# Statistics of every second tile of the last LayerNorm on ScalarE

## The chip, the cores and the metric

The kernel runs on one core of a Trainium2 chip. A time is the device time of one execution in microseconds; lower is better. It was taken in three runs, and one further execution was profiled.

## What is computed

One step of a streaming encoder layer for 1024 prompt tokens and 128 sample tokens with 1024 features: an input projection, three branches (a gated linear recurrence, stick-breaking attention, an mLSTM), their merging, a LayerNorm, a mixture of 32 experts of which each token takes four, and a second LayerNorm. The change concerns the second LayerNorm alone. In the reference it is the last line of the layer:

```
def _layer_norm(x, g, b):
    xf = x.astype(F32)
    mu = jnp.mean(xf, axis=-1, keepdims=True)
    var = jnp.mean(jnp.square(xf - mu), axis=-1, keepdims=True)
    return ((xf - mu) * lax.rsqrt(var + LN_EPS) * g.astype(F32) + b.astype(F32)).astype(x.dtype)
...
    x = _layer_norm(DN_ALPHA * x + f + ple, ln2_g, ln2_b)
```

All of it is computed in float32.

## The kernel before

The program is a row of stages. The last one, `stage_experts`, gathers the rows of each block of expert slots, multiplies them with that expert's two weights on TensorE, and adds the results with an indirect DMA to `residual_scratch` in DRAM, which then holds the sum `DN_ALPHA * x + f + ple`. When the last such DMA has landed, the class `LastNorm` works on the sum: 1152 tokens as NT = 9 tiles of 128 tokens (partitions) by 1024 features. Its tile `res` is the old place of the expert weights and of `xT` in on-chip memory, so the profile calls it `xT_then_expert_w`; the rows of gain and shift vectors (`norm`) stand in the first half of `expert_w`.

There is no planner. Each engine has its own instruction list, written out in program order, and semaphores tie the lists together:

- SyncE (`sync`) issues the nine loads of `res` one after the other, and then, for each tile, waits for `y_ready` and issues the store of that tile.
- VectorE (`vector`) makes, for each tile i, the statistics in `moments`: two `bn_stats` over 512 features each (L3788), one `bn_aggr` that gives mean and variance (L3791), then, once ScalarE has put the standard deviation in the variance's place, its reciprocal (L3793) and the shift -mean/std (L3796, a `scalar_tensor_tensor` of 128x1). After the moments of tile i it multiplies tile i-1 by the gain (L3807). So the statistics of a tile stand ahead of the gain of the tile before it.
- ScalarE (`scalar`) loads the table for the square root once and then makes, for each tile, the root of variance plus epsilon (L3824) and normalizes the tile in place (L3826: scale 1/std, bias -mean/std).
- GpSimd (`gpsimd`) adds the shift vector to each tile (L3815), after which the tile may be stored.

The tile `y` (`expert_y`) holds an expert block's results until they are added to DRAM. It is not used any more when `LastNorm` starts.

Of the kernel before, what the change touches and what calls it, by code (L numbers as in the profile page):

```python
# [29 lines left out]
ALU = mybir.AluOpType  # L30
ACT = mybir.ActivationFunctionType
AX_X = mybir.AxisListType.X

P = 128
D = 1024
# [5 lines left out]
NT = T // P  # L41
# [39 lines left out]
@contextmanager  # L81
def stage_semaphores(nc):

    owned = []

    def sem(name):
        owned.append(nc.alloc_semaphore(name))
        return owned[-1]

    yield sem  # L90
    nc.clear_and_free_semaphores(owned)
    nc.all_engine_barrier()
# [6 lines left out]
class WeightStream:  # L99
# [5 lines left out]
    def __init__(self, nc, ctx, g):  # L105
        self.nc = nc
        self.source = g.w_in[0].rearrange("(k p) n -> p k n", p=P)
        raw = ctx.enter_context(nc.sbuf_tensor("w_stream", [P, self.RAW * 512], F32, side="right"))
        hi = ctx.enter_context(nc.sbuf_tensor("w_stream_high", [P, self.WR * 512], F32R, side="right"))
        lo = ctx.enter_context(nc.sbuf_tensor("w_stream_low", [P, self.WR * 512], F32R, side="right"))  # L110
        self.raw, self.hi, self.lo = (t[:].rearrange("p (s n) -> p s n", n=512) for t in (raw, hi, lo))
        self.a_raw, self.a_hi, self.a_lo = (t[:, 0:3 * DT * P].rearrange("p (s k c) -> p s k c", s=3, k=DT)
                                            for t in (raw, hi, lo))
        sem = ctx.enter_context(stage_semaphores(nc))
        self.a_in = [sem(f"a_w_in{i}") for i in range(3)]
        self.a_high = sem("a_w_high")
        self.a_split = sem("a_w_split")
        self.a_done = sem("a_proj_done")
        self.v_in = [sem(f"v_w_in{i}") for i in range(self.RAW)]
        self.v_high = sem("v_w_high")  # L120
        self.v_split = sem("v_w_split")
        self.v_free = sem("v_w_free")
        self.m_prod = sem("m_prod")
        self.b_prod = sem("b_prod")
# [3145 lines left out]
def stage_experts(nc, g):  # L3270
# [20 lines left out]
    with ExitStack() as ctx:  # L3291
        sem = ctx.enter_context(stage_semaphores(nc))
        def sb(name, shape, dt=F32):
            return ctx.enter_context(nc.sbuf_tensor(name, shape, dt))
# [3 lines left out]
        w2 = sb("expert_w2", [P, FT, D])  # L3298
# [18 lines left out]
        y = sb("expert_y", [P, 2, D])  # L3317
# [28 lines left out]
        y_left = sem("e_y_left")  # L3346
        y_low = sem("e_y_low")
        waits_passed = sem("e_waits_passed")
        last_norm = LastNorm(nc, ctx, sem, g, w2[:, 0:2, :])
        block = ctx.enter_context(nc.Block())  # L3350

        def full_turns(eng):
# [390 lines left out]
class LastNorm:  # L3743


    def __init__(self, nc, ctx, sem, g, norm):
        def sb(name, shape):
            return ctx.enter_context(nc.sbuf_tensor(name, shape, F32))

        self.nc, self.g, self.norm = nc, g, norm  # L3750
        self.res = g.rows[:].rearrange("p (i d) -> p i d", i=NT)
        self.stats = sb("ln2_stats", [P, NT, 2, 6])
        self.mv = sb("ln2_mean_var", [P, NT, 2])
        self.shift = sb("ln2_shift", [P, NT, 1])
        self.root = sb("root_of_eps", [P, 1])
        self.norm_in = sem("k_norm_in")
        self.res_in = [sem(f"k_res_in{i}") for i in range(NT)]
        self.all_out = sem("k_all_out")
        self.stat_ready = sem("k_stat_ready")
        self.var_ready = sem("k_var_ready")  # L3760
        self.std_ready = sem("k_std_ready")
        self.rstd_ready = sem("k_rstd_ready")
        self.shift_ready = sem("k_shift_ready")
        self.hat_ready = sem("k_hat_ready")
        self.scaled = sem("k_scaled")
        self.y_ready = sem("k_y_ready")
        self.y_out = sem("k_y_out")
# [15 lines left out]

    def moments(self, dve, i):
        nc, mv = self.nc, self.mv
        dve.wait_ge(self.res_in[i], 16)
        for half in range(2):
            nc.vector.bn_stats(self.stats[:, i, half, :], self.res[:, i, half * 512:(half + 1) * 512]  # L3788
                               ).then_inc(self.stat_ready, 1)
        dve.wait_ge(self.stat_ready, 2 * i + 2)  # L3790
        nc.vector.bn_aggr(mv[:, i, :], self.stats[:, i].rearrange("p a b -> p (a b)")).then_inc(self.var_ready, 1)  # L3791
        dve.wait_ge(self.std_ready, i + 1)
        nc.vector.reciprocal(mv[:, i, 1:2], mv[:, i, 1:2]).then_inc(self.rstd_ready, 1)  # L3793

        dve.wait_ge(self.rstd_ready, i + 1)
        nc.vector.scalar_tensor_tensor(out=self.shift[:, i, :], in0=mv[:, i, 0:1], scalar=-1.0, in1=mv[:, i, 1:2],  # L3796
                                       op0=ALU.mult, op1=ALU.mult).then_inc(self.shift_ready, 1)

    def vector(self, dve):
        for i in range(NT + 1):  # L3800
            if i < NT:
                self.moments(dve, i)
            if i == 1:
                dve.wait_ge(self.norm_in, 32)
            if i:
                dve.wait_ge(self.hat_ready, i)
                self.nc.vector.tensor_tensor(self.res[:, i - 1, :], self.res[:, i - 1, :], self.norm[:, 0, :],  # L3807
                                             ALU.mult).then_inc(self.scaled, 1)
# [9 lines left out]
    def scalar(self, act):  # L3818
        nc, mv = self.nc, self.mv

        nc.scalar.activation(self.root[:], self.g.eps[:], ACT.Sqrt)
        for i in range(NT):
            act.wait_ge(self.var_ready, i + 1)
            nc.scalar.activation(mv[:, i, 1:2], mv[:, i, 1:2], ACT.Sqrt, bias=self.g.eps[:]).then_inc(self.std_ready, 1)  # L3824
            act.wait_ge(self.shift_ready, i + 1)
            nc.scalar.activation(self.res[:, i, :], self.res[:, i, :], ACT.Identity, bias=self.shift[:, i, :],  # L3826
                                 scale=mv[:, i, 1:2]).then_inc(self.hat_ready, 1)


def build_program(nc, i, o):  # L3830
# [20 lines left out]
    with ExitStack() as ctx:  # L3851
# [12 lines left out]
        with ExitStack() as trunk:  # L3864
# [14 lines left out]
            with ExitStack() as early:  # L3879
# [43 lines left out]
                with ExitStack() as pieces:  # L3923
# [6 lines left out]
                    stage_out(nc, g, xT, xT, out_early, route)  # L3930
                stage_route(nc, g, xT, route)
        stage_experts(nc, g)


# [20 lines left out]
```

## Time and profile before

| | us |
|---|---|
| three runs: median (lowest to highest) | 2656.44 (2656.16 to 2660.66) |
| profiled execution: its time | 2657.0 |
| profiled execution: span of its instructions | 2655.3 |
| start of the first load of `LastNorm`, from the span's start | 2607.39 |
| start of the first and end of the last GpSimd add | 2616.24, 2647.09 |

All times in the profile count from the span's start. An engine is busy while it executes an instruction; a wait inside an instruction counts as busy too. In the lists in order of time a row has start, duration, engine, line, operation, output and inputs, and in square brackets the time for which the engine was idle before it and what ended that. Starts and durations there are rounded to 0.01 us.

### The profile page before, as it was taken

The numbers are of one execution on the slowest core, as the hardware profiler recorded it, in microseconds if no ns is written. First come the engines' busy times: TensorE is split into PE (matmuls) and PEld (weight loads), VectorE is DVE, ScalarE is ACT, GpSimd is POOL, SyncE is SP. The second block draws the span as 40 slices with busy tenths as digits, with TensorE's granted clock in tenths as the row PEclk, the third lists the DMA queues.
The fourth block names the chain that finished last, engine by engine and source line by source line (L and its number), as shares of the span: only waits on it lengthen the run. The fifth ranks groups of instructions, "written<-read, shape, count | busy, mean of one in ns | idle before, by whom it ended". The sixth has DMA issues, their size and how long they took to land. (4 is left out here: it accounts for less than half of the span.)

```text
span 2655.3 us, 40268 instructions
## 1 busy us (share of the span) xinstructions
PE 2459.5 (93%) x14944; PEld 2220.1 (84%) x14944; DVE 1595.9 (60%) x2515; ACT 1313.5 (49%) x2098; POOL 671.3 (25%) x496
## 2 busy tenths in 40 slices
PE   7999999998878899999999989799999999999991
PEld 6988797896657899999988667688898999999991
DVE  3665331217658554444535476578788788877775
ACT  4566330115435544334322222467777677777662
POOL 1000100004302011010113214244444444544433
PEclk8999999999999899999999999899999999999995
DMA  8321233203387565565544322788998898988864
GB/s 249 90 67 43 80 100 104 83 20 127 110 292 180 127 163 134 131 163 141 136 123 148 124 77 75 242 280 276 288 289 280 275 280 283 292 259 282 275 195 170
DMA packets 389291, 468.10 MB, mean 176 GB/s; under 512 B 17326, under 2 KB 312458, under 8 KB 389167
## 3 DMA queue, kind: packets, MB, share of 16 engines
q1 hardware_dynamic: 367069, 395.82, 47.7%
q0 software_dynamic: 17760, 60.34, 9.0%
q10 hardware_dynamic: 4338, 10.23, 1.0%
q8 instruction: 85, 1.39, 0.2%
q14 instruction: 39, 0.32, 0.0%
HBM read 397.63 MB, written 68.71 MB: 176 GB/s over the span
## 5 line engine op out<-in xcount | busy, mean ns | idle before, releaser
L3523 PE MATMUL banks<-slot_rowsT,expert_w_high 128*128 128x288 f32 (+2 forms) x2048 | 561.4, 356 | 5.4 <-DVE expert_w_low L3661 4.7
L3526 PE MATMUL banks<-slot_rowsT,expert_w_low 128*128 128x144 f32 (+2 forms) x2048 | 494.0, 241 | 0.0
L3526 PEld LDWEIGHTS banks<-slot_rowsT,expert_w_low 128*128 128x128 f32 x2048 | 399.9, 195 | 1.4
L3523 PEld LDWEIGHTS banks<-slot_rowsT,expert_w_high 128*128 128x128 f32 x2048 | 394.2, 192 | 7.5 <-DVE expert_w_low L3661 5.0
L3577 ACT CAST expert_w_high<-xT_then_expert_w 128x2048 fp32r<-128x2048 f32 x127 | 235.6, 1903 | 2.9 <-DMA xT_then_expert_w<-in_exp_w 2.9
L3661 DVE TENSOR_TENSOR expert_w_low<-xT_then_expert_w,expert_w_high 128x2048 fp32r<-128x2048 f32 x95 | 214.5, 2285 | 17.0 <-ACT expert_w_high L3577 17.0
L3444 POOL TENSOR_TENSOR expert_w_low<-xT_then_expert_w,expert_w_high 128x2048 fp32r<-128x2048 f32 x32 | 146.6, 4582 | 207.5 <-ACT expert_w_high L3577 207.5
L2246 PE MATMUL banks<-xT_chunk_high,w_gates_high 128*128 128x384 f32 x576 | 193.7, 336 | 4.5 <-DVE xT_chunk_low L2318 4.5
L2247 PE MATMUL banks<-xT_chunk_low,w_gates_high 128*128 128x384 f32 x576 | 193.5, 336 | 0.0
L2248 PE MATMUL banks<-xT_chunk_high,w_gates_low 128*128 128x384 f32 x576 | 193.4, 336 | 0.0
L3702 DVE TENSOR_TENSOR expert_w_low<-expert_w,expert_w_high 128x1024 fp32r<-128x1024 f32 x128 | 159.2, 1243 | 51.7 <-ACT expert_w_high L3605 51.7
L2366 POOL TENSOR_TENSOR xT_then_expert_w<-xT_then_expert_w,gate_sigmoid 128x384 f32<-128x384 f32 x48 | 56.5, 1176 | 488.4 <-DVE gate_sigmoid L2357 488.4
L3594 ACT ACTIVATE low_part_and_bias<-banks,expert_b 128x192 f32<-128x192 f32 x256 | 93.8, 418 | 108.0 <-PE banks L3526 107.7
L2283 ACT CAST w_gates_high<-w_gates 128x1024 fp32r<-128x1024 f32 x72 | 75.7, 1052 | 130.9 <-PE banks L2258 130.0
L3469 POOL DMA_INDIRECT residual_scratch<-expert_y,slot_rows_out x64 | 123.2, 1924 | 49.0 <-POOL slot_rows_out L3437 28.2
L3605 ACT CAST expert_w_high<-expert_w 128x1024 fp32r<-128x1024 f32 x128 | 132.2, 1033 | 1.0 <-DMA expert_w<-in_exp_w 1.0
L2258 PE MATMUL banks<-yT_chunk_high,w_proj_low 128*128 128x384 f32 x384 | 128.3, 334 | 0.0
L2256 PE MATMUL banks<-yT_chunk_high,w_proj_high 128*128 128x384 f32 x384 | 128.3, 334 | 0.0
L2257 PE MATMUL banks<-yT_chunk_low,w_proj_high 128*128 128x384 f32 x384 | 128.3, 334 | 0.0
L2333 DVE TENSOR_TENSOR w_gates_low<-w_gates,w_gates_high 128x1024 fp32r<-128x1024 f32 x72 | 109.2, 1516 | 31.4 <-ACT w_gates_high L2283 31.2
L3688 DVE TENSOR_TENSOR gate_and_up<-banks,low_part_and_bias 128x384 f32<-128x384 f32 x128 | 71.0, 555 | 93.9 <-ACT low_part_and_bias L3594 93.3
L2357 DVE TENSOR_TENSOR gate_sigmoid<-gate_sigmoid,banks 128x384 f32<-128x384 f32 x48 | 26.6, 554 | 160.8 <-PE banks L2258 160.8
(552 smaller groups left out, 6184.0 us busy)
## 6 DMA issues: line engine op xcount, KB each, us to landing
xT_then_expert_w<-in_exp_w SPq DMA_DIRECT2D x126, 1024.0 KB, 7.8
expert_w<-in_exp_w SPq DMA_DIRECT2D x32, 2048.0 KB, 9.4
w_gates<-in_w_in SPq DMA_DIRECT2D x72, 512.0 KB, 4.4
cached_k<-in_cache_sb_k SPq DMA_DIRECT2D x16, 1024.0 KB, 10.1
cached_v<-in_cache_sb_v SPq DMA_DIRECT2D x16, 1024.0 KB, 10.2
w_stream<-in_w_in SPq DMA_DIRECT2D x48, 256.0 KB, 4.2
w_proj<-in_w_pa SPq DMA_DIRECT2D x24, 512.0 KB, 5.1
w_stream<-in_w_in SPq DMA_DIRECT2D x16, 512.0 KB, 5.4
```

The source lines that it names most:

```text
L2246: nc.tensor.matmul(gate, hi, x_hi[:, k, :], start=(k == 0), stop=False)
L2247: nc.tensor.matmul(gate, hi, x_lo[:, k, :], start=False, stop=False)
L2248: last = nc.tensor.matmul(gate, lo, x_hi[:, k, :], start=False, stop=(k == DT - 1))
L2256: nc.tensor.matmul(proj, hi, y_hi[:, first + k, :], start=(k == 0), stop=False)
L2257: nc.tensor.matmul(proj, hi, y_lo[:, first + k, :], start=False, stop=False)
L3444: pool.tensor_tensor(w1_chunk(w1_lo, FT - 1), w1_chunk(w1, FT - 1), w1_chunk(w1_hi, FT - 1).bitcast(F32), ALU.subtract).then_inc(w1_last_s ...
L3523: nc.tensor.matmul(out[:, 0:2 * SLOTS].rearrange("p (a s) -> p a s", a=2)[:, :, 0:width], hi, xgT[:, par, k, :, 0:width], start=(place == ...
L3526: last = nc.tensor.matmul(out[:, 0:width], lo, xgT[:, par, k, 0, 0:width], start=False, stop=(place == DT - 1), skip_group_check=True)
L3577: nc.scalar.copy(w1_chunk(w1_hi, f), w1_chunk(w1, f)).then_inc(w1_high, 1)
L3605: nc.scalar.copy(w2_hi[:, f, :], w2[:, f, :]).then_inc(w2_high, 1)
L3661: nc.vector.tensor_tensor(w1_chunk(w1_lo, f), w1_chunk(w1, f), w1_chunk(w1_hi, f).bitcast(F32), ALU.subtract).then_inc(w1_split, 1)
L3702: nc.vector.tensor_tensor(w2_lo[:, f, :], w2[:, f, :], w2_hi[:, f, :].bitcast(F32), ALU.subtract).then_inc(w2_split, 1)
```

## The change

For odd tiles (1, 3, 5, 7) the statistics move from VectorE to ScalarE. ScalarE reads the tile with an identity activation that also sums along the features, turns the sum into -mean with a 128x1 copy, and reads the tile again with a square activation whose bias is -mean and which also sums; the root of the odd tile then takes this sum with scale 1/1024. The passes' elementwise output goes to `y[:, 0, :]` and is not read. Since an odd tile's mean has its sign turned, its shift is taken with +1 instead of -1. Even tiles keep `bn_stats` and `bn_aggr` on VectorE.

The order on both engines changes too. On VectorE `moments` is split: `factors(i)` (reciprocal and shift) comes first, then the statistics of tile i+1 (only if that is even), and then the gain of tile i-1. On ScalarE the two passes of tile i+1 stand between the root of an even tile i and its normalizing.

```diff
-        last_norm = LastNorm(nc, ctx, sem, g, w2[:, 0:2, :])
+        last_norm = LastNorm(nc, ctx, sem, g, w2[:, 0:2, :], y[:, 0, :])
...
+        self.sums = sb("ln2_sums", [P, NT, 2])
+        self.pass_out = pass_out
...
     def moments(self, dve, i):
         nc, mv = self.nc, self.mv
-        dve.wait_ge(self.res_in[i], 16)
-        for half in range(2):
-            nc.vector.bn_stats(...)
-        dve.wait_ge(self.stat_ready, 2 * i + 2)
-        nc.vector.bn_aggr(mv[:, i, :], ...).then_inc(self.var_ready, 1)
+        if i % 2 == 0:
+            dve.wait_ge(self.res_in[i], 16)
+            for half in range(2):
+                nc.vector.bn_stats(...)
+            dve.wait_ge(self.stat_ready, i + 2)
+            nc.vector.bn_aggr(mv[:, i, :], ...).then_inc(self.var_ready, 1)
+
+    def factors(self, dve, i):
+        nc, mv = self.nc, self.mv
         dve.wait_ge(self.std_ready, i + 1)
         nc.vector.reciprocal(mv[:, i, 1:2], mv[:, i, 1:2]).then_inc(self.rstd_ready, 1)
         dve.wait_ge(self.rstd_ready, i + 1)
-        nc.vector.scalar_tensor_tensor(out=self.shift[:, i, :], in0=mv[:, i, 0:1], scalar=-1.0, ...)
+        nc.vector.scalar_tensor_tensor(out=self.shift[:, i, :], in0=mv[:, i, 0:1], scalar=1.0 if i % 2 else -1.0, ...)
 
     def vector(self, dve):
+        self.moments(dve, 0)
         for i in range(NT + 1):
             if i < NT:
-                self.moments(dve, i)
+                self.factors(dve, i)
+            if i + 1 < NT:
+                self.moments(dve, i + 1)
             if i == 1:
                 dve.wait_ge(self.norm_in, 32)
             if i:
                 dve.wait_ge(self.hat_ready, i)
...
         nc.scalar.activation(self.root[:], self.g.eps[:], ACT.Sqrt)
+        def sums(i):
+            act.wait_ge(self.res_in[i], 16)
+            nc.scalar.activation(self.pass_out, self.res[:, i, :], ACT.Identity, accum_out=self.sums[:, i, 0:1]
+                                 ).then_inc(self.sum_ready, 1)
+            act.wait_ge(self.sum_ready, i)
+            nc.scalar.activation(mv[:, i, 0:1], self.sums[:, i, 0:1], ACT.Copy, scale=-1.0 / D
+                                 ).then_inc(self.mean_ready, 1)
+            act.wait_ge(self.mean_ready, i // 2 + 1)
+            nc.scalar.activation(self.pass_out, self.res[:, i, :], ACT.Square, bias=mv[:, i, 0:1],
+                                 accum_out=self.sums[:, i, 1:2]).then_inc(self.sum_ready, 1)
         for i in range(NT):
-            act.wait_ge(self.var_ready, i + 1)
-            nc.scalar.activation(mv[:, i, 1:2], mv[:, i, 1:2], ACT.Sqrt, bias=self.g.eps[:]).then_inc(self.std_ready, 1)
+            if i % 2 == 0:
+                act.wait_ge(self.var_ready, i // 2 + 1)
+                nc.scalar.activation(mv[:, i, 1:2], mv[:, i, 1:2], ACT.Sqrt, bias=self.g.eps[:]
+                                     ).then_inc(self.std_ready, 1)
+                if i + 1 < NT:
+                    sums(i + 1)
+            else:
+                act.wait_ge(self.sum_ready, i + 1)
+                nc.scalar.activation(mv[:, i, 1:2], self.sums[:, i, 1:2], ACT.Sqrt, bias=self.g.eps[:], scale=1.0 / D
+                                     ).then_inc(self.std_ready, 1)
             act.wait_ge(self.shift_ready, i + 1)
             nc.scalar.activation(self.res[:, i, :], self.res[:, i, :], ACT.Identity, bias=self.shift[:, i, :],
                                  scale=mv[:, i, 1:2]).then_inc(self.hat_ready, 1)
```

## Rows read from the trace of the kernel before

**Rows 1.** The page, busy time, share of the span and instructions of each engine

```profile
PE 2459.5 (93%) x14944; PEld 2220.1 (84%) x14944; DVE 1595.9 (60%) x2515; ACT 1313.5 (49%) x2098; POOL 671.3 (25%) x496
```

**Rows 2.** Table by stretches: stretch, its length, busy us (instructions) of each engine

```profile
2607.39:2616.24 8.85, 0.00 (x0) 0.00 (x0) 4.85 (x12) 3.07 (x4) 0.00 (x1) 0.50 0.86 322
2616.24:2647.09 30.85, 0.00 (x0) 0.00 (x0) 25.25 (x43) 10.75 (x14) 21.06 (x9) 0.50 0.49 197
```

**Rows 3.** Instructions in order of time, one turn of the last norm

```profile
2619.65 1.27 DVE L3788 BATCH_NORM_STATS2 ln_stats<-xT_then_expert_w 128x6 f32<-128x512 f32 x2
2619.81 2.34 POOL L3815 TENSOR_TENSOR xT_then_expert_w<-xT_then_expert_w,expert_w 128x1024 f32<-128x1024 f32 x1 [1.23 <-DVE xT_then_expert_w L3807]
...
2621.53 0.16 DVE L3793 RECIPROCAL ln_mean_var<-ln_mean_var 128x1 f32<-128x1 f32 x1 [0.36 <-ACT ln_mean_var L3824]
2621.73 0.44 DVE L3796 SCALAR_TENSOR_TENSOR ln_shift<-ln_mean_var 128x1 f32<-128x1 f32 x1
2622.09 1.21 DVE L3807 TENSOR_TENSOR xT_then_expert_w<-xT_then_expert_w,expert_w 128x1024 f32<-128x1024 f32 x1
...
2623.23 1.27 DVE L3788 BATCH_NORM_STATS2 ln_stats<-xT_then_expert_w 128x6 f32<-128x512 f32 x2
2623.38 2.34 POOL L3815 TENSOR_TENSOR xT_then_expert_w<-xT_then_expert_w,expert_w 128x1024 f32<-128x1024 f32 x1 [1.23 <-DVE xT_then_expert_w L3807]
```

**Rows 4.** Instructions in order of time, before the first add

```profile
2612.09 0.29 ACT L3824 ACTIVATE ln_mean_var<-ln_mean_var,ln_eps 128x1 f32<-128x1 f32 x1 [11.62 <-DVE ln_mean_var L3791]
...
2612.69 1.28 DVE L3788 BATCH_NORM_STATS2 ln_stats<-xT_then_expert_w 128x6 f32<-128x512 f32 x2
...
2614.86 1.23 DVE L3807 TENSOR_TENSOR xT_then_expert_w<-xT_then_expert_w,expert_w 128x1024 f32<-128x1024 f32 x1
...
2616.24 2.34 POOL L3815 TENSOR_TENSOR xT_then_expert_w<-xT_then_expert_w,expert_w 128x1024 f32<-128x1024 f32 x1 [13.20 <-DVE xT_then_expert_w L3807]
```

**Rows 5.** Line L3796: count, ns least/median/most, first and last start

```profile
L3796 DVE SCALAR_TENSOR_TENSOR ln_shift<-ln_mean_var x9: 159/439/515, 2612.6 to 2639.6; 128x1 f32<-128x1 f32 x9
```

**Rows 6.** Instructions in order of time, the last multiply

```profile
2641.25 2.34 POOL L3815 TENSOR_TENSOR xT_then_expert_w<-xT_then_expert_w,expert_w 128x1024 f32<-128x1024 f32 x1 [1.23 <-DVE xT_then_expert_w L3807]
2641.34 3.33 DVE L3807 TENSOR_TENSOR xT_then_expert_w<-xT_then_expert_w,expert_w 128x1024 f32<-128x1024 f32 x1 [0.17 <-ACT xT_then_expert_w L3826]
```

**Rows 7.** Chain of waits in order of time: start, us on the chain, what

```profile
2622.17 1.14 DVE xT_then_expert_w L3807
2623.30 1.21 DVE ln_stats L3788 x2
...
2624.53 0.22 DVE ln_mean_var L3791
```

**Rows 8.** ScalarE by line from 2598 on: count, busy us, mean ns, idle before

```profile
L3826 ACT ACTIVATE xT_then_expert_w<-xT_then_expert_w,ln_shift,ln_mean_var 128x1024 f32<-128x1024 f32 x9 | 11.2, 1241 | 5.9 <-DVE ln_shift L3796 5.9
L3824 ACT ACTIVATE ln_mean_var<-ln_mean_var,ln_eps 128x1 f32<-128x1 f32 x9 | 2.6, 294 | 21.2 <-DVE ln_mean_var L3791 21.2
L3821 ACT ACT_TABLE_LOAD x1 | 1.3, 1283 | 0.0
L3637 ACT ACTIVATE expert_y<-banks,slot_gates 128x512 f32<-128x512 f32 x2 | 1.3, 683 | 0.0
L3821 ACT ACTIVATE root_of_eps<-ln_eps 128x1 f32<-128x1 f32 x1 | 0.2, 203 | 0.0
```

**Rows 9.** The page's costliest groups: the cast of expert weights on ScalarE

```profile
L3605 ACT CAST expert_w_high<-expert_w 128x1024 fp32r<-128x1024 f32 x128 | 132.2, 1033 | 1.0 <-DMA expert_w<-in_exp_w 1.0
```

**Rows 10.** Instructions in order of time, an earlier stage

```profile
958.20 1.01 POOL L2366 TENSOR_TENSOR xT_then_expert_w<-xT_then_expert_w,gate_sigmoid 128x384 f32<-128x384 f32 x1 [5.57 <-DVE gate_sigmoid L2357]
958.23 2.06 DVE L2333 TENSOR_TENSOR w_gates_low<-w_gates,w_gates_high 128x1024 fp32r<-128x1024 f32 x1
```

**Rows 11.** Line L2333: count, ns least/median/most, first and last start

```profile
L2333 DVE TENSOR_TENSOR w_gates_low<-w_gates,w_gates_high x72: 1212/1717/2065, 877.7 to 1365.9; 128x1024 fp32r<-128x1024 f32 x72
```

**Rows 12.** The nine loads of the last norm (L3776)

```profile
DMA to landing us min/median/max: 4.2/8.1/10.4
```

More of the change, by code:

```diff
@@ L3743, with __init__ @@
 class LastNorm:
-    def __init__(self, nc, ctx, sem, g, norm):
+    def __init__(self, nc, ctx, sem, g, norm, pass_out):
         def sb(name, shape):
@@ L3755, in __init__ @@
         self.root = sb("root_of_eps", [P, 1])
+        self.sums = sb("ln2_sums", [P, NT, 2])
+        self.pass_out = pass_out
+        self.sum_ready = sem("k_sum_ready")
+        self.mean_ready = sem("k_mean_ready")
         self.norm_in = sem("k_norm_in")
@@ L3785, in moments @@
         nc, mv = self.nc, self.mv
-        dve.wait_ge(self.res_in[i], 16)
-        for half in range(2):
-            nc.vector.bn_stats(self.stats[:, i, half, :], self.res[:, i, half * 512:(half + 1) * 512]
-                               ).then_inc(self.stat_ready, 1)
-        dve.wait_ge(self.stat_ready, 2 * i + 2)
-        nc.vector.bn_aggr(mv[:, i, :], self.stats[:, i].rearrange("p a b -> p (a b)")).then_inc(self.var_ready, 1)
+        if i % 2 == 0:
+            dve.wait_ge(self.res_in[i], 16)
+            for half in range(2):
+                nc.vector.bn_stats(self.stats[:, i, half, :], self.res[:, i, half * 512:(half + 1) * 512]
+                                   ).then_inc(self.stat_ready, 1)
+            dve.wait_ge(self.stat_ready, i + 2)
+            nc.vector.bn_aggr(mv[:, i, :], self.stats[:, i].rearrange("p a b -> p (a b)")).then_inc(self.var_ready, 1)
+    def factors(self, dve, i):
+        nc, mv = self.nc, self.mv
         dve.wait_ge(self.std_ready, i + 1)
@@ L3795, in moments @@
         dve.wait_ge(self.rstd_ready, i + 1)
-        nc.vector.scalar_tensor_tensor(out=self.shift[:, i, :], in0=mv[:, i, 0:1], scalar=-1.0, in1=mv[:, i, 1:2],
-                                       op0=ALU.mult, op1=ALU.mult).then_inc(self.shift_ready, 1)
+        nc.vector.scalar_tensor_tensor(out=self.shift[:, i, :], in0=mv[:, i, 0:1], scalar=1.0 if i % 2 else -1.0,
+                                       in1=mv[:, i, 1:2], op0=ALU.mult, op1=ALU.mult).then_inc(self.shift_ready, 1)
     def vector(self, dve):
+        self.moments(dve, 0)
         for i in range(NT + 1):
             if i < NT:
-                self.moments(dve, i)
+                self.factors(dve, i)
+            if i + 1 < NT:
+                self.moments(dve, i + 1)
             if i == 1:
```

## The prediction

> **What bounds the kernel now.** I read the page's head first, then three stretches of the end, then the chain of waits, then the end's instructions in order of time, and last single lines. The page's head is the frame and a trap: TensorE is busy for 93% of the span [rows 1], but this change lies wholly behind its last matmul. The table by stretches shows that end [rows 2]: 8.85 us from the first load's issue to GpSimd's first add, 30.85 us in which the nine adds run, and behind them the last store and the closing. No TensorE work is in either, so what is added there is added to the time one for one.
>
> In the 30.85 us VectorE is busy for 25.25 and GpSimd for 21.06 [rows 2]; VectorE looks like the bound. The instructions in order of time say otherwise. One tile's turn is 3.57 us: GpSimd's adds start at 2619.81 and 2623.38 [rows 3]. Inside it the statistics of the next tile run beside the add and are over early; VectorE's tiny `ln_shift` (L3796, 128x1) starts at 2621.73, takes 0.44 instead of 0.16, and ends at 2622.17, when the add that began at 2619.81 ends (2622.15) [rows 3]. Over all nine the median is 439 ns, the least 159 [rows 5]. The last gain multiply (L3807) shows the same at full size: it begins 0.09 after an add and takes 3.33, ending 1.08 after that add, where others take 1.21 [rows 3, 6]. `bn_stats` (1.27) and the reciprocal (0.16) keep their durations under the add (two statistics took 1.28 where none was running) [rows 3, 4]. So a VectorE instruction with two SBUF inputs stands still while GpSimd adds, and one with a single input doesn't. The turn is add 2.34, end of the shift 0.02, multiply 1.14 (from the shift's end, as the chain of waits has it), hand-over 0.08: 3.58 [rows 3, 7]. Nine adds and eight such steps of 1.24 are 31.0 against 30.85 in rows 2. The bound is add and multiply taking turns on something that both need; the statistics hide under the add.
>
> **The change part by part.** Four tiles (1, 3, 5, 7) lose two `bn_stats` and one aggregate on VectorE: 1.21 + 0.24 each in the chain [rows 7]. For tiles 3, 5 and 7 that work lay under an add, so its removal is worth nothing by itself. ScalarE gains for each a summing pass, a 128x1 copy and a squaring pass. VectorE's order changes too: before, `moments(i)` was statistics, reciprocal, shift of one tile; now the reciprocal and shift of tile i+1 stand ahead of the statistics of tile i+2. This reordering is what costs.
>
> *The filling.* The first multiply now waits for tile 1's factors, whose statistics ScalarE makes after tile 0's root at 2612.38 [rows 4]. No row has a pass with a summed output. Its bounds are the 128x1024 cast without operand pointers, 1.03 [rows 9], and the normalizing pass with two, 1.24 [rows 8], each possibly with one more 128x1 activation for the sum, 0.29 [rows 4]; I take 1.13 for the sum and 1.14 for the square, since the instructions have the cast's size and at most one pointer. The copy lies between 0.20 [rows 8] and 0.29; I take 0.25. The steps, with 0.03 at each hand-over (the shift starts 0.04 after the reciprocal's end, 2621.69 [rows 3]): sum 1.13, copy 0.28, square 1.17, tile 0's normalizing 1.14 and tile 1's root 0.19 (each started 0.1 early, as two evictions of 683 ns are busy for 1.3 together [rows 8]), reciprocal 0.19, shift 0.19, tile 2's `bn_stats` 1.21 and aggregate 0.24, multiply 1.14, hand-over 0.08. Sum 6.96; the first add stood 0.15 behind its multiply instead of 0.08 [rows 4], which is 0.07 more, and I allow 0.2 for two or three waits of ScalarE on itself, which no row has: the first add starts at about 2612.38 + 7.23 = 2619.6, where it started at 2616.24. Filling: +3.4. With passes of 1.03 and no such allowance it is +3.0, with passes of 1.24 + 0.29 it is +4.2. Tile 1's load is there by then: its `bn_stats` at 2612.69 met no wait [rows 4], so the pass at 2612.4 waits at most 0.3.
>
> *The turns.* After the multiply of tile i-1 VectorE goes straight to the reciprocal and the shift of tile i+1. An instruction without a wait starts 0.08 before the multiply's end is recorded (2623.23 against 2623.30) [rows 3]; the reciprocal takes 0.16 and the hand-over 0.03, so the shift starts 0.12 after the multiply's end, and the add 0.08 after it. The shift is 0.04 late. In the nearest case in this trace a VectorE subtraction started 0.03 after a GpSimd product (958.23 against 958.20) and took 2.06 [rows 10], where its line's least is 1212 ns [rows 11]. So the shift loses: it waits for the add's end. That hurts nobody where no statistics follow. Where i+2 is even, `bn_stats` and aggregate of tile i+2 are queued behind the blocked shift; they can run only after the add, and the next multiply, and with it the next add, is behind them. What lay under the add for nothing is now on the path at 1.21 + 0.24 = 1.45 [rows 7]. This happens for the statistics of tiles 4, 6 and 8; tile 2's is in the filling. 3 x 1.45 = +4.35. If the pairs overlap a little it is 1.40, if the multiply starts afresh 1.53: 4.2 to 4.6.
>
> The Trainium skill, "SBUF — State Buffer", section "SBUF: two separate sides", has a rule for such a meeting: whichever of GpSimd and a VectorE instruction with two SBUF inputs starts first keeps their common port for its whole length. The 2.06 agrees with it. By the rule the recorded starts alone decide, and 0.04 late gives the sum below in every turn; by the row alone no more is known than that 0.03 late was lost once.
>
> For an odd tile i+1 the loss is surer: its root comes behind the even tile's normalizing pass, which waits for that tile's shift, so its reciprocal starts some 0.4 after the multiply.
>
> *ScalarE* has room. Between an even tile's aggregate and its shift's end lie multiply 1.14, hand-over 0.08, add 2.34 and 0.02, in all 3.58; root, sum, copy and square need 2.9. A further 1.8 is free because the odd tile's shift must wait for the next add's end anyway. So 2.5 us of dearer passes in each pair would cost nothing in the turns, only in the filling.
>
> *The end.* The last multiply waits for tile 8's normalizing, which waits for a shift that no statistics precede: it starts just behind the add of tile 7 as before and stands still once [rows 6]. Store and closing are as before. The loads landed 4.2 to 10.4 after their issue, half of them within 8.1 [rows 12]. Only tile 3 is wanted sooner than before, at some 2618.5 instead of 2619.65 [rows 3]; as the fourth of nine issued one after the other from 2607.39 [rows 2] it should be there.
>
> **Sum.** +3.4 + 4.35 = +7.75, from +7.2 to +8.8. The profiled execution took 2657.0 (span 2655.3 and 1.7 around it), so 2664.75; the median of the three runs, 2656.44, lies 0.56 lower, so 2664.2.
>
> **Rivals.**
>
> *The shift slips in ahead of the add.* Then the statistics run under the add as before, and odd tiles' factors are in time as well, since ScalarE's pair of tiles takes 0.29 + 2.58 + 1.14 + 0.19 + 1.24 = 5.4 of 7.15 us. Only the filling remains: 2656.4 + 3.4 = 2659.8, which is +0.13% and so not slower by the bound that I use: 0.2%, 5.3 us, about what a measurement of this kernel can tell from no change. For it: 0.04 us is little, and it decides as soon as the shift starts no later than the add takes hold. Against it: 0.03 late was lost [rows 10].
>
> *VectorE's own time is the bound after all.* Then the three odd turns shrink until GpSimd's add limits them, from 3.57 to 2.42: 3 x 1.15 = -3.45, which the filling of +3.4 eats: 2656.4, no change. For it: VectorE's 25.25 busy of 30.85 [rows 2]. Against it: 0.28 of each shift is waiting, and the 3.33 of the last multiply. The Trainium skill's "Perfetto Trace Analysis", section "Optimizing Scalar/DVE Operations", advises moving work to ScalarE when VectorE is saturated, and warns of its shared port with GpSimd; by its first half this rival would come, by its warning mine.
>
> *The table is loaded anew for the squaring pass and again for the root.* Two loads of 1.283 [rows 8] for each odd tile: 2.57 in the filling, and 0.1 above the 2.5 free in each of three turns, so some +2.8 more: 2667.0. Against it: nine identity passes alternate with nine roots behind a single load in this stretch [rows 8]; no square is seen there. The Trainium skill's "ScalarE: Activation LUTs", section "Table sets: the hidden batching unit", says that cheap functions are in every set, which speaks against this rival.
>
> **Numbers.** The forecast 0.72, the shift in time 0.13, VectorE as bound 0.05, tables 0.07, something unseen 0.03. The forecast alone would be 2663.2 to 2665.6; with tables it reaches 2667. Leaving out the rival at 2659.8 would leave out more than 0.2, so the range is 2659.3 to 2667.3. Slower by over 0.2%: the forecast less the tenth of it that scatter may push under 5.3 us, and tables: 0.74. Within 0.2%: 0.23. Faster: 0.03, since no case reaches -5.3.
>
> **What the profile after would show.** First add near 2619.6. GpSimd's adds 3.57 and 5.0 us apart by turns, three times 5.0. Shifts of 1.7 to 2.3 us, each ending with an add. `bn_stats` of tiles 4, 6, 8 after the add and not beside it. No table load after L3821's. I am wrong if all distances are 3.57 (the shift was in time), if they are under 3.5 in odd turns (VectorE was the bound), or if ScalarE's passes exceed 1.5.

## The result and the profile after

The changed kernel is slower. Its median over 19 runs is 2661.21 us, that of the kernel before over 19 runs beside it 2656.16, which is 5.05 less. The ratio of the two kernels, formed from all these runs, is 1.0026 with a 95% interval from 1.0014 to 1.0037, which is 6.9 us, from 3.7 to 9.8. The forecast was +7.75; the range held the median and the sign was right. That the kernel is slower by over 0.2% is likely but not shown, since 1.002 lies inside the interval.

The page's head of the profiled execution:

```profile
span 2664.3 us, 40276 instructions
...
PE 2459.5 (92%) x14944; PEld 2218.4 (83%) x14944; DVE 1602.8 (60%) x2503; ACT 1323.9 (50%) x2118; POOL 668.7 (25%) x496
```

The span grew by 9.0, but not all of that is the change's. The first load of the last norm is issued at 2609.20, where it was issued at 2607.39 before, and nothing ahead of it differs in the program: in the profiled executions of this study that moment lies anywhere from 2599.32 to 2612.63. So the runs below are compared by the stretch from that issue to the end of the last full-size instruction of the norm, and by the closing behind it, both read from the trace. Before, the stretch is 39.70 [rows 2], now it is 46.86. That is +7.15 (before rounding).

The table by stretches of the changed kernel, cut as in [rows 2] at the first add:

```profile
2609.20:2621.11 11.91, 0.00 (x0) 0.00 (x0) 4.77 (x13) 6.55 (x12) 0.00 (x1) 0.50 0.92 355
2621.11:2656.06 34.95, 0.00 (x0) 0.00 (x0) 31.32 (x30) 16.53 (x28) 21.07 (x9) 0.50 0.34 134
```

The filling grew from 8.85 to 11.91 (+3.06), the stretch of the nine adds from 30.85 to 34.95 (+4.10). GpSimd's busy time is the same 21.07: its adds aren't slower, they stand further apart. VectorE's instructions in that stretch fell from 43 to 30 [rows 2], and yet it is busy for 31.32 instead of 25.25. The busy time that came is waiting, as the order in time shows, here two turns in place of the one in [rows 3]:

```profile
2628.32 1.17 DVE L3818 TENSOR_TENSOR xT_then_expert_w<-xT_then_expert_w,expert_w 128x1024 f32<-128x1024 f32 x1
...
2629.41 0.15 DVE L3801 RECIPROCAL ln_mean_var<-ln_mean_var 128x1 f32<-128x1 f32 x1
2629.57 2.34 POOL L3826 TENSOR_TENSOR xT_then_expert_w<-xT_then_expert_w,expert_w 128x1024 f32<-128x1024 f32 x1 [2.62 <-DVE xT_then_expert_w L3818]
...
2629.60 2.34 DVE L3804 SCALAR_TENSOR_TENSOR ln_shift<-ln_mean_var 128x1 f32<-128x1 f32 x1
...
2631.86 1.21 DVE L3818 TENSOR_TENSOR xT_then_expert_w<-xT_then_expert_w,expert_w 128x1024 f32<-128x1024 f32 x1
...
2633.15 2.34 POOL L3826 TENSOR_TENSOR xT_then_expert_w<-xT_then_expert_w,expert_w 128x1024 f32<-128x1024 f32 x1 [1.24 <-DVE xT_then_expert_w L3818]
2633.43 0.16 DVE L3801 RECIPROCAL ln_mean_var<-ln_mean_var 128x1 f32<-128x1 f32 x1 [0.36 <-ACT ln_mean_var L3855]
2633.63 1.88 DVE L3804 SCALAR_TENSOR_TENSOR ln_shift<-ln_mean_var 128x1 f32<-128x1 f32 x1
2635.43 1.27 DVE L3793 BATCH_NORM_STATS2 ln_stats<-xT_then_expert_w 128x6 f32<-128x512 f32 x2
...
2636.74 0.21 DVE L3796 BATCH_NORM_AGGREGATE ln_mean_var<-ln_stats 128x2 f32<-128x12 f32 x1
2636.86 1.17 DVE L3818 TENSOR_TENSOR xT_then_expert_w<-xT_then_expert_w,expert_w 128x1024 f32<-128x1024 f32 x1
...
2638.12 2.34 POOL L3826 TENSOR_TENSOR xT_then_expert_w<-xT_then_expert_w,expert_w 128x1024 f32<-128x1024 f32 x1 [2.62 <-DVE xT_then_expert_w L3818]
```

The adds that start at 2629.57, 2633.15 and 2638.12 are 3.58 and 4.97 apart. In both turns the shift (L3804) stands still until the add ends, 2.34 and 1.88 long for a 128x1 result. Behind the first the multiply follows at once. Behind the second come the statistics of an even tile, 2635.43 to 2636.95, beside nothing: the next multiply starts at 2636.86. In [rows 3] the same statistics ran beside the add. Line L3804 as a whole, to be held against [rows 5]:

```profile
L3804 DVE SCALAR_TENSOR_TENSOR ln_shift<-ln_mean_var x9: 158/1879/2339, 2614.4 to 2646.7; 128x1 f32<-128x1 f32 x9
```

The median shift went from 439 to 1879 ns, with only the three that start ahead of the first add at 0.16.

### The profile page after: what moved, and what is told of

Its sections match the earlier page's. It is cut to its first block and busy times, and to the rows that moved or that the text cites. A ratio compares the mean times of both kernels' runs of the same rounds, so it can differ in the third digit from the quotient of the medians.

```text
span 2664.3 us, 40276 instructions
## 1 busy us (share of the span) xinstructions
PE 2459.5 (92%) x14944; PEld 2218.4 (83%) x14944; DVE 1602.8 (60%) x2503; ACT 1323.9 (50%) x2118; POOL 668.7 (25%) x496
## 3 DMA queue, kind: packets, MB, share of 16 engines
q8 instruction: 85, 1.39, 0.2%
## 5 line engine op out<-in xcount | busy, mean ns | idle before, releaser
L2333 DVE TENSOR_TENSOR w_gates_low<-w_gates,w_gates_high 128x1024 fp32r<-128x1024 f32 x72 | 109.2, 1517 | 31.5 <-ACT w_gates_high L2283 31.2
## 6 DMA issues: line engine op xcount, KB each, us to landing
cached_k<-in_cache_sb_k SPq DMA_DIRECT2D x16, 1024.0 KB, 10.4
cached_v<-in_cache_sb_v SPq DMA_DIRECT2D x16, 1024.0 KB, 10.4
```

## The experiments

All numbers are of one profiled execution of each; the ratio to the kernel before is over several runs. Distances are between the starts of successive adds.

| run | first load to first add | distances between adds | stretch | closing | ratio to before (95%) |
|---|---|---|---|---|---|
| before | 8.85 | 3.57, last 3.50 | 39.70 | 8.19 | |
| the change | 11.91 | 3.51, then 4.96 and 3.57 by turns, last 3.50 | 46.86 | 8.22 | 1.0026 (1.0014 to 1.0037) |
| e1, order alone | 10.34 | 3.51, five of 4.96, 3.57, 3.50 | 48.05 | 8.19 | 1.0043 (1.0025 to 1.0062) |
| e2, offload alone | 10.59 | 3.57 to 3.58, last 3.50 | 41.47 | 8.22 | 1.0021 (1.0007 to 1.0034) |
| e3, shift with one input | 12.13 | 3.50 to 3.52, last 3.22 | 42.25 | 8.22 | 1.0012 (0.9997 to 1.0026) |
| e4, tiles 3, 5, 7 only | 8.98 | 3.57 to 3.58, last 3.50 | 39.86 | 8.22 | 0.9997 (0.9984 to 1.0011) |
| e5, gain in PSUM, before | 9.17 | 3.27, six of 3.34, 2.30 | 37.13 | 8.21 | 0.9990 (0.9978 to 1.0002) |
| e6, gain in PSUM, change | 12.08 | 2.32 and 3.67 to 3.76 by turns, last 2.32 and 2.30 | 37.19 | 8.22 | 1.0000 (0.9985 to 1.0015) |
| e7, two fused passes | no adds | | 30.29 | 4.40 | 0.9956 (0.9942 to 0.9971) |
| e8, e7 without offload | no adds | | 40.69 | 4.40 | 0.9995 (0.9981 to 1.0008) |
| e9, two adds on VectorE | 8.90 | 3.57 to 3.58 (seven adds) | 37.49 | 4.40 | 0.9979 (0.9967 to 0.9991) |

**e1: the order alone.** The two halves of the change were taken apart. Here VectorE's new order, without the sums and squares on ScalarE:

```diff
     def vector(self, dve):
+        self.moments(dve, 0)
         for i in range(NT + 1):
             if i < NT:
-                self.moments(dve, i)
+                self.factors(dve, i)
+            if i + 1 < NT:
+                self.moments(dve, i + 1)
```

> The kernel before (all statistics on VectorE, no passes on ScalarE) with only the change's order on VectorE: reciprocal and shift of tile i+1 ahead of the statistics of tile i+2. Measured by the stretch from the issue of the first load to the end of the last GpSimd add: 39.70 us before, 46.86 us with the whole change. Theory (the shift stands still under the add and the statistics are queued behind it): the statistics of tile 2 come into the filling (+1.45) and those of tiles 3 to 8 each lie between an add and the next multiply, 6 x 1.39; six distances between adds of 4.96, stretch about 49.4, some 0.35% slower than before. Rival (ScalarE's two passes are what makes the turns of 4.96): without the passes every distance stays at 3.57, stretch about 41.2.

One turn of it in order of time:

```profile
2630.18 1.17 DVE L3813 TENSOR_TENSOR xT_then_expert_w<-xT_then_expert_w,expert_w 128x1024 f32<-128x1024 f32 x1
...
2631.43 2.34 POOL L3821 TENSOR_TENSOR xT_then_expert_w<-xT_then_expert_w,expert_w 128x1024 f32<-128x1024 f32 x1 [2.62 <-DVE xT_then_expert_w L3813]
2631.46 2.33 DVE L3799 SCALAR_TENSOR_TENSOR ln_shift<-ln_mean_var 128x1 f32<-128x1 f32 x1
2633.71 1.27 DVE L3788 BATCH_NORM_STATS2 ln_stats<-xT_then_expert_w 128x6 f32<-128x512 f32 x2
...
2635.14 1.17 DVE L3813 TENSOR_TENSOR xT_then_expert_w<-xT_then_expert_w,expert_w 128x1024 f32<-128x1024 f32 x1
...
2636.40 2.34 POOL L3821 TENSOR_TENSOR xT_then_expert_w<-xT_then_expert_w,expert_w 128x1024 f32<-128x1024 f32 x1 [2.62 <-DVE xT_then_expert_w L3813]
```

The add runs from 2631.43 to 2633.77, the shift beside it stands still, and the statistics and the multiply come one after the other behind it: 4.97 to the next add. Five turns were so long and not six: the first shift behind a multiply got ahead of the first add (the reason stands below), so tile 3's statistics were still covered. The stretch is 48.05, 1.4 under the 49.4 expected for that reason, and far from the rival's 41.2. The new order makes the long turns without any sums or squares on ScalarE.

**e2: the offload alone.** The other half: passes on ScalarE as in the change, VectorE's order as before.

```diff
     def vector(self, dve):
-        self.moments(dve, 0)
         for i in range(NT + 1):
             if i < NT:
+                self.moments(dve, i)
                 self.factors(dve, i)
-            if i + 1 < NT:
-                self.moments(dve, i + 1)
```

> The change's passes on ScalarE, with VectorE's order as before: statistics, reciprocal and shift of tile i, then the gain of tile i-1. Theory (order): no distance of 4.96, all near 3.57; the filling loses tile 2's statistics, 11.9 - 1.45 = 10.5; stretch about 41.3, 1.6 above the kernel before (0.06%, not to be told by time). Rival (ScalarE's passes make the turns long): three distances of 4.96 stay, stretch about 45.4.

A turn in order of time, add, shift, add:

```profile
2617.06 2.35 POOL L3824 TENSOR_TENSOR xT_then_expert_w<-xT_then_expert_w,expert_w 128x1024 f32<-128x1024 f32 x1 [1.23 <-DVE xT_then_expert_w L3816]
...
2618.98 0.45 DVE L3804 SCALAR_TENSOR_TENSOR ln_shift<-ln_mean_var 128x1 f32<-128x1 f32 x1
...
2620.64 2.35 POOL L3824 TENSOR_TENSOR xT_then_expert_w<-xT_then_expert_w,expert_w 128x1024 f32<-128x1024 f32 x1 [1.23 <-DVE xT_then_expert_w L3816]
```

The distance is 3.58, and no turn is longer. The stretch is 41.47, 1.77 above the kernel before, nearly all of it in the filling (10.59 against 8.85). With the closing that is +1.8, 0.07%, which is the lower end of the measured interval.

**e3: the shift with one SBUF tensor.** One instruction differs from the changed kernel:

```diff
-        nc.vector.scalar_tensor_tensor(out=self.shift[:, i, :], in0=mv[:, i, 0:1], scalar=1.0 if i % 2 else -1.0,
-                                       in1=mv[:, i, 1:2], op0=ALU.mult, op1=ALU.mult)
+        nc.vector.tensor_scalar(self.shift[:, i, :], mv[:, i, 0:1], mv[:, i, 1:2], 1.0 if i % 2 else -1.0,
+                                ALU.mult, ALU.mult)
```

> The changed kernel with one instruction of each tile altered: the shift is a tensor_scalar with one SBUF tensor (the mean) and 1/std as a per-partition scalar, instead of a scalar_tensor_tensor with two. Order and passes stay. Theory (an instruction with two SBUF inputs stands still under the add, one with a single tensor doesn't): shifts take 0.2 everywhere, the statistics of tiles 4, 6 and 8 run under the add, distances 3.57; filling stays at 11.9; stretch about 42.7, 4.1 less than the change. Rival (VectorE's order costs whatever the shift does, or the per-partition scalar counts as a second input): shifts up to 2.3, distances of 4.96, stretch 46.9.

VectorE's multiply and shift by line (count, busy us, mean ns):

```profile
L3818 DVE TENSOR_TENSOR xT_then_expert_w<-xT_then_expert_w,expert_w 128x1024 f32<-128x1024 f32 x9 | 21.0, 2341 | 0.0
...
L3804 DVE TENSOR_SCALAR ln_shift<-ln_mean_var 128x1 f32<-128x1 f32 x9 | 1.9, 214 | 0.3
```

All nine shifts take 0.21, whether an add runs or not, and the waiting has moved to the multiply, which now takes 2.34 on average. The statistics of even tiles run under the add again, and the stretch fell by 4.6 to 42.25, a little more than the 4.1 expected, since the distances are 3.51 and not 3.57. What is left over the kernel before, 2.55, is the filling (+3.3) less the shorter distances (-0.7). So in the turns the order costs only because of how this one 128x1 instruction reads its operands. In the filling it costs whatever the shift does: 11.91 with the new order against 10.59 without it (e2), and 12.13 here.

The last distance, 3.22, shows the same meeting the other way round: here the last multiply starts 0.16 ahead of the add and takes 1.21, and it is the add that stands still, 3.25 instead of 2.34.

**e4: three tiles, order as before.** Tile 1 keeps its statistics on VectorE; tiles 3, 5 and 7 have theirs on ScalarE.

```diff
-        if i % 2 == 0:
+        if i not in (3, 5, 7):
             dve.wait_ge(self.res_in[i], 16)
```

(with the counts that the semaphores are waited for, and VectorE's order as in e2)

> VectorE's order as before, passes on ScalarE for tiles 3, 5 and 7 only; tile 1 keeps its statistics on VectorE. Theory (add and multiply take turns, statistics lie under the add): filling as before, 8.85, distances 3.57, stretch 39.7: taking statistics from VectorE is worth nothing. Rival (VectorE's own work is the bound): the three turns without statistics fall towards 2.42, stretch about 36.3.

39.86 against 39.70, every distance as before. Three tiles' statistics, 4.3 us of VectorE's work, were taken away for no gain. But this run alone doesn't say why. One of the three turns without statistics, in order of time:

```profile
2623.10 2.35 POOL L3824 TENSOR_TENSOR xT_then_expert_w<-xT_then_expert_w,expert_w 128x1024 f32<-128x1024 f32 x1 [1.24 <-DVE xT_then_expert_w L3816]
...
2625.11 0.16 DVE L3801 RECIPROCAL ln_mean_var<-ln_mean_var 128x1 f32<-128x1 f32 x1 [2.09 <-ACT ln_mean_var L3853]
2625.30 0.16 DVE L3804 SCALAR_TENSOR_TENSOR ln_shift<-ln_mean_var 128x1 f32<-128x1 f32 x1
```

VectorE is idle for 2.09 here because ScalarE's root of the odd tile comes late, and the shift starts only 0.15 before the add ends (0.22 in the first of the three turns). So ScalarE's passes would have held these turns near 3.57 even if nothing stood still. What settles it is the changed kernel's turn from 2629.57 to 2633.15, shown above: it has no statistics, its reciprocal waits for nothing, VectorE's own work in it is some 1.5, and it is 3.58 long all the same, since the shift stands still until the add ends. VectorE's own work is not the bound.

**e5: the gain vector in PSUM.** ScalarE copies the gain vector to a free pair of banks of PSUM, the on-chip memory beside SBUF, ahead of the norm, so that the multiply reads one tensor from SBUF and one from PSUM; the shift is that of e3; all else is the kernel before.

```diff
+        act.wait_ge(self.norm_in, 32)
+        for half in range(2):
+            nc.scalar.copy(self.g.bank[half][:], self.norm[:, 0, half * 512:(half + 1) * 512]).then_inc(self.gain_moved, 1)
...
-                self.nc.vector.tensor_tensor(self.res[:, i - 1, :], self.res[:, i - 1, :], self.norm[:, 0, :],
+                self.nc.vector.tensor_tensor(self.res[:, i - 1, :], self.res[:, i - 1, :], self.gain,
```

> The kernel before (all statistics on VectorE, its order) with the gain vector copied to PSUM by ScalarE ahead of the norm, so that the multiply has one SBUF input and one PSUM input, and the shift as in the run before with one SBUF tensor. Theory (two SBUF inputs are what excludes GpSimd's add): the multiply runs beside the add with some 1.25, a turn is VectorE's own chain, statistics 1.45, root 0.32, reciprocal 0.19, shift 0.2, multiply 1.2, together 3.35; the last multiply takes 1.25 instead of 3.33; stretch 8.9 + 8 x 3.35 + 2.34 = 38.0. Rival (any full-size VectorE instruction is held up by the add): distances stay at 3.5 and the last multiply at 3.3; stretch 39.5.

A shift and a multiply within a turn, and the end (two adds back to back, with the last multiply beside them), in order of time:

```profile
2622.71 0.21 DVE L3798 TENSOR_SCALAR ln_shift<-ln_mean_var 128x1 f32<-128x1 f32 x1
2622.84 1.21 DVE L3809 TENSOR_TENSOR xT_then_expert_w<-xT_then_expert_w,banks 128x1024 f32<-128x1024 f32 x1
...
2634.16 4.64 POOL L3817 TENSOR_TENSOR xT_then_expert_w<-xT_then_expert_w,expert_w 128x1024 f32<-128x1024 f32 x2 [1.00 <-DVE xT_then_expert_w L3809]
2634.26 1.22 DVE L3809 TENSOR_TENSOR xT_then_expert_w<-xT_then_expert_w,banks 128x1024 f32<-128x1024 f32 x1 [0.18 <-ACT xT_then_expert_w L3831]
```

The last multiply starts 0.10 after an add, as in [rows 6], and takes 1.22 instead of 3.33. The distances are 3.34, the time of the chain from statistics to multiply, all of it on VectorE but for ScalarE's root. It is the two SBUF inputs that exclude the add, not the size of the instruction.

**e6: the same two edits in the changed kernel.**

> The changed kernel with the same two edits (gain in PSUM, shift with one SBUF tensor). Theory: with add and multiply no longer excluding each other VectorE needs 4.7 for a pair of tiles and GpSimd 4.85, and ScalarE becomes the bound with 5.9 for a pair (two roots, sum, copy, square, two normalizing passes, two waits for a shift): 2.95 for a tile; stretch 11.9 + 8 x 2.95 + 2.34 = 37.8, 9 less than the change and 1.9 less than the kernel before. So the change's offload would then pay. Rival (the exclusion lies elsewhere): as with the one-input shift alone, 42.3.

Two of the pairs of adds in order of time (each row two adds back to back):

```profile
2621.59 4.67 POOL L3828 TENSOR_TENSOR xT_then_expert_w<-xT_then_expert_w,expert_w 128x1024 f32<-128x1024 f32 x2 [1.32 <-DVE xT_then_expert_w L3820]
...
2627.67 4.66 POOL L3828 TENSOR_TENSOR xT_then_expert_w<-xT_then_expert_w,expert_w 128x1024 f32<-128x1024 f32 x2 [1.41 <-DVE xT_then_expert_w L3820]
```

Two adds run back to back, then GpSimd waits 1.4 for the next pair: 6.08 from pair to pair, 3.04 for a tile, where 2.95 was expected. ScalarE alone doesn't hold a pair: it is idle for 0.68 of it, and the 6.08 are a loop of ScalarE's root, sum, copy, square, normalizing pass and root (4.2) and VectorE's reciprocal, shift and statistics behind them (1.9). The stretch is 37.19 against 37.8 expected, less because the last three adds run back to back; it is 9.7 under the change and 2.5 under the kernel before, though the ratio, 1.0000, doesn't show so small a gain. But e5 gets the same 37.1 without any offload: the shorter turns here (3.04 against 3.34) are eaten by the longer filling (12.08 against 9.17).

**e7: two fused passes, no add on GpSimd.** Since add and multiply take turns at 2.34 + 1.14, the add is cheaper on VectorE itself, and with mean and 1/std as per-partition scalars the normalizing pass goes as well.

```diff
+            nc.vector.scalar_tensor_tensor(out=self.res[:, i, :], in0=self.res[:, i, :], scalar=mv[:, i, 0:1],
+                                           in1=self.norm[:, 0, :], op0=ALU.subtract if i in self.ON_DVE else ALU.add,
+                                           op1=ALU.mult).then_inc(self.scaled, 1)
...
+            nc.vector.scalar_tensor_tensor(out=self.res[:, i, :], in0=self.res[:, i, :], scalar=mv[:, i, 1:2],
+                                           in1=self.norm[:, 1, :], op0=ALU.mult, op1=ALU.add).then_inc(self.y_ready, 1)
```

> A version that removes GpSimd's add: VectorE makes two scalar_tensor_tensor passes for each tile, (x - mean) * gain and then (that * 1/std) + shift vector; ScalarE makes no normalizing pass but sums and squares of all tiles except 0 and 4, whose statistics VectorE makes; GpSimd does nothing in the norm. Same outputs. Theory: nothing contends with VectorE, whose work is 9 x (1.14 + 0.17 + 1.14) + 2 x 1.45 = 25; ScalarE 7 x 3.0 = 21 is beside it but sets when a tile may start; from the issue of the first load to the last VectorE pass about 28.5, against 39.7 before and 46.9 with the change; 0.4% faster than before. Rival (a pass with a per-partition scalar and two inputs is dearer than the multiply, up to twice): stretch 39 or more.

The two passes by line:

```profile
L3819 DVE SCALAR_TENSOR_TENSOR xT_then_expert_w<-xT_then_expert_w,ln_mean_var,expert_w 128x1024 f32<-128x1024 f32 x9 | 11.6, 1285 | 0.3
L3812 DVE SCALAR_TENSOR_TENSOR xT_then_expert_w<-xT_then_expert_w,ln_mean_var,expert_w 128x1024 f32<-128x1024 f32 x9 | 11.5, 1275 | 0.6 <-ACT expert_y L3845 0.6
```

30.29 against 28.5 expected. A fused pass is recorded with 1.28, of which the next instruction overlaps 0.08; from start to start it takes 1.20 where 1.14 was put in, some 1.1 for eighteen, and VectorE waits twice for ScalarE, 0.55 together. The closing is shorter by 3.8 as well, which was not expected. Together 13.2 less than before; measured, the ratio is 0.9956, 11.7 us (7.7 to 15.4). It beats both kernels.

**e8: e7 with all statistics on VectorE.** `ON_DVE` holds all nine tiles, and ScalarE makes roots only.

> The version with two fused VectorE passes, but with the statistics of all nine tiles on VectorE and none on ScalarE: what the offload is worth once VectorE is the bound. Theory (VectorE's own work sets this version's time): 3.2 to the first statistics and 9 x (1.45 + 1.24 + 0.12 + 1.28 and 0.1 for waits) = 38, stretch about 41, against 30.3 with seven tiles on ScalarE: the same passes that were worth nothing beside GpSimd's add are worth some 10 us. Rival (the gain of the fused version is the missing add and the shorter closing, not the offload): stretch near 31.

40.69, 10.4 over e7. Here VectorE is the bound, and the passes on ScalarE, which beside GpSimd's adds were worth nothing, are worth 10.4.

**e9: the last two adds on VectorE.** The kernel before, to find out about the closing.

```diff
+                if i > NT - 2:
+                    dve.wait_ge(self.scaled, i)
+                    self.nc.vector.tensor_tensor(self.res[:, i - 1, :], self.res[:, i - 1, :], self.norm[:, 1, :],
+                                                 ALU.add).then_inc(self.y_late, 1)
...
-        for i in range(NT):
+        for i in range(NT - 2):
             pool.wait_ge(self.scaled, i + 1)
```

> The kernel before with the adds of the last two tiles (7 and 8) on VectorE instead of GpSimd. In the trace before, the closing takes 8.19 from the last add's end to the span's end, and GpSimd's own drain lasts until 2653.7, 4.0 after the last store has landed; in the version without adds it takes 4.4 from the last VectorE pass. Theory (the closing waits for GpSimd to drain some 6.6 after its last full-size instruction): last work ends 2.2 earlier, as multiplies and adds of 1.2 follow one another on VectorE, and the closing falls from 8.2 to 4.4; 6.0 in all, 0.2%. Rival (the shorter closing came from something else, such as the GpSimd wait on the vectors or the stores): closing stays at 8.2, gain 2.2.

Stretch 37.49 and closing 4.40: 5.99 less than before in all, as expected; the ratio is 0.9979.

## Why the prediction was right

**What bounds the norm.** Right. A turn of the changed kernel with some 1.5 of work on VectorE is still 3.58 long, and e5 removes the second SBUF input with all the work left on VectorE, and the turn falls from 3.57 to 3.34, with the last multiply at 1.22. It falls no further because the chain through the statistics was only 0.23 shorter than add and multiply in turns. e4, meant as the test of this, agrees but can't decide it, since ScalarE held its three turns as well.

**The turns.** Right in place and mechanism, a little too dear. Three distances grew by 1.39 each and not by 1.45 (the prediction named 1.40 for pairs that overlap): with no wait between them the multiply starts some 0.1 before the aggregate ends (2636.86 against 2636.95). e1 and e2 split the change: the order alone makes the long turns, the offload alone makes none. e3 removes them by one instruction's operands. The recorded starts decided each time: shifts recorded 0.03 after the add's start stood still, as at 2631.46 in e1 and at 2629.60 in the change, and the add of e3 that was recorded 0.16 after a multiply's start stood still too. The Trainium skill, "SBUF — State Buffer", section "SBUF: two separate sides", says that whichever starts first keeps the shared port; these starts agree with it. The rival that the shift slips in ahead came true in one turn, the first:

```profile
2619.77 1.18 DVE L3818 TENSOR_TENSOR xT_then_expert_w<-xT_then_expert_w,expert_w 128x1024 f32<-128x1024 f32 x1
...
2621.06 0.16 DVE L3804 SCALAR_TENSOR_TENSOR ln_shift<-ln_mean_var 128x1 f32<-128x1 f32 x1
2621.11 2.35 POOL L3826 TENSOR_TENSOR xT_then_expert_w<-xT_then_expert_w,expert_w 128x1024 f32<-128x1024 f32 x1 [16.20 <-DVE xT_then_expert_w L3818]
2621.14 3.40 DVE L3818 TENSOR_TENSOR xT_then_expert_w<-xT_then_expert_w,expert_w 128x1024 f32<-128x1024 f32 x1
```

The first hand-over to GpSimd was 0.16 instead of 0.08, as [rows 4] had shown for the kernel before, so the add started at 2621.11, 0.05 behind the shift. The shift took 0.16, and tile 1's multiply, 0.03 behind the add, stood still in its place (3.40). The prediction used the long first hand-over in the filling and forgot it here. That changed one distance only, to 3.51 from 3.57, since no statistics were queued behind that shift.

**The filling.** Right in its steps, 0.35 too much: 3.06 against 3.4. The chain of waits of the changed kernel:

```profile
2614.16 1.05 ACT expert_y L3837 x2
...
2615.23 0.21 ACT ln_mean_var L3840
...
2615.47 1.24 ACT expert_y L3843 x2
2616.71 1.13 ACT xT_then_expert_w L3858
2617.84 0.20 ACT ln_mean_var L3855
...
2618.26 0.16 DVE ln_shift L3804
2618.41 1.21 DVE ln_stats L3793 x2
...
2619.77 1.18 DVE xT_then_expert_w L3818
```

ScalarE's passes, by line (count, busy us, mean ns):

```profile
L3843 ACT ACTIVATE expert_y<-xT_then_expert_w,ln_mean_var 128x1024 f32<-128x1024 f32 x4 | 4.6, 1148 | 0.1
L3837 ACT ACTIVATE expert_y<-xT_then_expert_w 128x1024 f32<-128x1024 f32 x4 | 4.2, 1040 | 0.0
...
L3843 ACT ACTIVATION_READ_ACCUMULATOR expert_y<-xT_then_expert_w,ln_mean_var 128x1 f32 x4 | 0.7, 186 | 0.0
```

The summing pass takes 1.04, the squaring pass 1.15, and the sums are read by an instruction of their own of 0.19, which starts 0.1 before the pass ends. The chain carries 1.05 and 1.24, together 2.29, where the forecast had 1.13 + 1.14 and 0.03 twice. Their total was right partly by luck, since the sum was 0.08 too dear and the square 0.10 too cheap; too much were the 0.2 allowed for ScalarE's waits on itself, which did not come, and 0.1 at the aggregate.

**The other rivals.** VectorE as the bound fell with the turn of 3.58 and e5, as said above. No table load stands among ScalarE's instructions in this stretch, so identity and square run on the table of the root.

**Sum.** 3.06 in the filling and 4.10 in the turns make 7.15 (before rounding) against 7.75. The time alone would not have shown the mechanism: the median, 2661.21, lies 3.0 under the forecast of 2664.2, outside the 2663.2 to 2665.6 that the forecast alone allowed, and only 1.4 above the rival's 2659.8, in which the shift slips in ahead. It fell into the range because that rival had been let in. The distances between the adds tell the two apart: three of 4.96, where the rival has none.

## What to carry to other kernels

Where GpSimd and VectorE pass a tile back and forth in SBUF, count an instruction of VectorE with two SBUF inputs as a barrier, however small it is, and put nothing behind it that could have run beside GpSimd's instruction. An engine's busy share doesn't say that relieving it helps: take work away only after seeing which of its instructions wait. And give a tiny instruction one tensor and a per-partition scalar where that computes the same.

## What the runs showed of the hardware beside this

The closing waits for GpSimd. Behind its last instruction GpSimd drains, and all engines meet after that: in the kernel before, the semaphore rows of all of them at the end start at 2653.8 to 2653.9. Drains of GpSimd and SyncE in the kernel before (duration ns, start us):

```profile
L3291 POOLq DRAIN  x1: 9002/9002/9002, 2644.7 to 2644.7; - x1
...
L3291 SPq DRAIN  x1: 7/7/7, 2649.9 to 2649.9; - x1
```

GpSimd's in e7, where it does nothing in the norm:

```profile
L3291 POOLq DRAIN  x1: 6598/6598/6598, 2600.1 to 2600.1; - x1
```

And in e9, where its last add is tile 6's:

```profile
L3291 POOLq DRAIN  x1: 9011/9011/9011, 2638.7 to 2638.7; - x1
...
L3291 SPq DRAIN  x1: 7/7/7, 2648.7 to 2648.7; - x1
```

Before, SyncE is done at 2649.9, when the last store is in, but GpSimd's drain lasts until 2644.7 + 9.0 = 2653.7, 6.6 after its last add has ended at 2647.09. In e9 it starts with tile 6's add at 2638.7 and is over at 2647.7, ahead of SyncE, and the closing falls from 8.19 to 4.40. The drain alone in e7 is 6.6 too. What GpSimd does in those 6.6 the runs don't show.
